# Encoder kernel, layer A: loads and norm in one block, and memory keys and values made in float32 in two places

## The chip, the cores and the metric

The kernel runs on one core of a Trainium2 chip. The metric is the device time of one execution in microseconds (us), as the median of several; less is better. The span is what the profiler sees of one execution, from its first to its last instruction.

## What is computed

```python
def layer_a(x, mem, ln_g, w_in, mem_ln_g, w_mem, w_out):
    h = rms_norm(x, ln_g)
    z = h @ w_in
    ...
    y_mix = dilated_mixer(qkv).astype(x.dtype)
    y_mem = memory_attention(q_mem, rms_norm(mem, mem_ln_g), w_mem)
    y = jnp.concatenate([y_mix, y_mem], axis=-1) * jax.nn.silu(gate)
    return x + y @ w_out

def memory_attention(q, mem_n, w_mem):
    kv = mem_n @ w_mem
    kh = kv[..., :MEM_WIDTH].reshape(Bn, M, MEM_HEADS, HEAD_DIM)
    vh = kv[..., MEM_WIDTH:].reshape(Bn, M, MEM_HEADS, HEAD_DIM)
    s = jnp.einsum('bshe,bmhe->bhsm', qh, kh).astype(F32) * (HEAD_DIM ** -0.5)
    p = jax.nn.softmax(s, axis=-1)
    o = jnp.einsum('bhsm,bmhe->bshe', p.astype(vh.dtype), vh)
```

Two sequences (prompt and sample) of 512 tokens with 1024 features go through layer A (three dilated attentions and an attention over 256 memory rows per sequence) and layer B (gated linear attention and the same memory attention with weights of its own), and a last norm. The memory attention has 4 heads of 128.

## The kernel before

Tokens and features stand transposed, features in the 128 partitions, in 8 chunks of 128 (`KC`). All is float32. The large products are not made in float32 but with every operand split into a high and a low part of type fp32r: ScalarE (ACT) copies the high part, VectorE (DVE) or GpSimd (POOL) subtracts it from the operand to get the low one, and TensorE (PE) makes three products, high by high, high by low, low by high. Small products (scores, transposes, weighted values) are plain float32 matmuls; the profile counts two MATMUL records for each of them, but one for a transpose.

The order is written out by hand, engine by engine, with semaphores. Stages are blocks: a stage begins when all engines and the queues have ended the one before.

1. `load_and_transpose`. SP loads 12 tiles of 128 rows, four of memory and then eight of tokens, into three buffers. PE transposes each, ACT squares it for the sum of squares (L391), and ACT (L392) and DVE (L400) each move a half out of PSUM. The memory tiles are scaled by their norm on DVE (L417). POOL issues the loads of the five gains and of `onorm` (L346, L347), which add to the semaphore `const_in`. SP stores both to DRAM (L334, L337).
2. `norm_a`. DVE computes the norm factors of all 8 token tiles, spreads them over the partitions with PE (L657, L625), scales the tokens (L639), and forms sums of token quarters, since the projection uses a Strassen-like scheme with 7 products for 8 (`OPS`). ACT makes the high parts (L601), DVE and POOL share the low parts (L587) and the sums, and PE makes the 7 products of the first pair of weight columns (L301 to L303).
3. `dilated`. 44 pairs of columns, 7 products each; attention is woven in. The last four pairs belong to the memory heads: their queries and gates.
4. `memory_a`. SP loads the normed memory; DVE multiplies each chunk by the gain (L1386), ACT and DVE split it (L1319, L1389). For each head PE makes keys and values transposed (`unit`, L198 to L200, four times 24 matmuls of width 256), ACT moves them out (L1298), PE turns the values (L1229). For each of four groups of 256 queries: scores (L1210), softmax on DVE and ACT (L1344 to L1356, L1277), transposes of the probabilities (L1221), and per sequence the weighted values (L1237). DVE multiplies by the gate (L1364) and SP stores y (L1188).
5. The output projection of layer A begins (L1749, L1801), then layer B, whose memory stage `memory_b` has the same steps as 4 (gain: L1679, low part: L1682).

## Time and profile before

| | us |
|---|---|
| median of 3 runs | 2252.23 |
| lowest and highest | 2248.18, 2253.43 |
| the profiled execution | 2254.23 |
| its span | 2252.6 |
| PE busy | 2094.9 (93%) |
| DVE busy | 1177.1 (52%) |
| ACT busy | 839.6 (37%) |
| POOL busy | 525.8 (23%) |

Busy time counts instructions, not waits. PE's ends are modelled, so its share is an upper bound. A stage can be far from the mean: what bounds it is read from the waits in it. The granted clock of PE has two levels, 1.2 and 2.4 GHz, shown as 0.5 and 1.0 of full speed.

### The profile page before, as it was taken

Reading aid. Unit: us, or ns where it says so; the run is one execution under the profiler, and the core shown is the slowest. Engines: PE = TensorE matmul, PEld = TensorE weight load, DVE = VectorE, ACT = ScalarE, POOL = GpSimd, SP = SyncE. Lnnn points to the kernel's source line nnn. Section 1 sums busy time; section 2 is a strip of 40 time slices with the busy share of each in tenths; the row PEclk is TensorE's granted clock in tenths of the full one; section 3 lists DMA queues with packets and bytes.
Section 4 is the critical chain, followed back from the end, with each engine's and each line's share of the span. In section 5 each row is a group of like instructions: output and inputs, shape, how many; then the busy total and the mean of one; then the engine's idle time right before and its main releaser. Section 6 shows DMA issues by size and latency. Waiting matters only on the chain. (4 is left out here: it accounts for less than half of the span.)

```text
span 2252.6 us, 29111 instructions
## 1 busy us (share of the span) xinstructions
PE 2094.9 (93%) x10172; PEld 1707.4 (76%) x10172; DVE 1177.1 (52%) x2047; ACT 839.6 (37%) x1518; POOL 525.8 (23%) x394
## 2 busy tenths in 40 slices
PE   5799999999999999999987998999898987998998
PEld 4578888787888788888776786778787875886786
DVE  6755464647363645555344434576868583433423
ACT  5333443434253434343344312343434442334310
POOL 4623232323232222323100023132323231000010
PEclk7899999999999999999989998999999998999998
DMA  7122222121112112212123522210101012222612
GB/s 263 42 57 62 57 57 70 47 70 52 61 51 74 47 59 59 64 56 62 54 91 103 160 67 101 71 29 20 57 19 56 19 37 75 63 60 63 189 56 93
DMA packets 210834, 157.21 MB, mean 70 GB/s; under 512 B 8625, under 2 KB 196305, under 8 KB 210514
## 3 DMA queue, kind: packets, MB, share of 16 engines
q1 hardware_dynamic: 205842, 147.68, 21.7%
q0 software_dynamic: 4928, 8.70, 1.6%
q8 instruction: 37, 0.61, 0.1%
q14 instruction: 27, 0.22, 0.0%
HBM read 128.99 MB, written 27.36 MB: 69 GB/s over the span
## 5 line engine op out<-in xcount | busy, mean ns | idle before, releaser
L274 DVE TENSOR_TENSOR w_lo<-w_raw,w_hi 128x512 fp32r<-128x512 f32 x303 | 271.8, 898 | 354.6 <-ACT w_hi L270 354.0
L198 PE MATMUL z_ps<-b_parts,w_hi 128*128 128x512 f32 x656 | 271.0, 413 | 20.4 <-ACT g_gate L208 12.3
L270 ACT ACTIVATE w_hi<-w_raw 128x512 fp32r<-128x512 f32 x308 | 192.5, 626 | 229.3 <-PE z_ps L303 101.6
L200 PE MATMUL z_ps<-b_parts,w_lo 128*128 128x512 f32 x656 | 265.4, 405 | 0.0
L301 PE MATMUL z_ps<-ah_hi,w_hi 128*128 128x512 f32 x608 | 249.1, 410 | 11.6 <-DVE ah_lo L587 9.0
L303 PE MATMUL z_ps<-ah_hi,w_lo 128*128 128x512 f32 x608 | 243.2, 400 | 0.0
L302 PE MATMUL z_ps<-ah_lo,w_hi 128*128 128x512 f32 x608 | 242.4, 399 | 0.0
L199 PE MATMUL z_ps<-b_parts,w_hi 128*128 128x512 f32 x560 | 228.0, 407 | 0.0
L183 DVE TENSOR_TENSOR w_lo<-w_raw,w_hi 128x1024 fp32r<-128x1024 f32 (+1 forms) x65 | 119.4, 1837 | 140.4 <-ACT w_hi L179 139.9
L198 PEld LDWEIGHTS z_ps<-b_parts,w_hi 128*128 128x128 f32 x656 | 128.5, 196 | 55.2 <-issue 25.2
L2121 POOL TENSOR_TENSOR g_E<-g_E,g_q 128x1024 f32<-128x1024 f32 x28 | 91.2, 3259 | 292.1 <-ACT g_E L2323 278.1
L301 PE MATMUL t_ps<-ah_hi,w_hi 128*128 128x512 f32 x352 | 144.6, 411 | 8.0 <-DVE ah_lo L587 6.6
L200 PEld LDWEIGHTS z_ps<-b_parts,w_lo 128*128 128x128 f32 x656 | 127.8, 195 | 30.6
L301 PEld LDWEIGHTS z_ps<-ah_hi,w_hi 128*128 128x128 f32 x608 | 116.1, 191 | 39.4 <-issue 10.8
L303 PE MATMUL t_ps<-ah_hi,w_lo 128*128 128x512 f32 x352 | 140.4, 399 | 0.0
L302 PE MATMUL t_ps<-ah_lo,w_hi 128*128 128x512 f32 x352 | 140.3, 399 | 0.0
L303 PEld LDWEIGHTS z_ps<-ah_hi,w_lo 128*128 128x128 f32 x608 | 115.9, 191 | 27.8
L302 PEld LDWEIGHTS z_ps<-ah_lo,w_hi 128*128 128x128 f32 x608 | 116.5, 192 | 25.2
L249 POOL TENSOR_TENSOR w_raw<-w_raw 128x512 f32<-128x512 f32 x44 | 57.1, 1298 | 322.9 <-DMA w_raw<-in_a_win 316.7
L199 PEld LDWEIGHTS z_ps<-b_parts,w_hi 128*128 128x128 f32 x560 | 110.0, 196 | 23.6
L736 ACT ACTIVATE qkv<-z_ps 128x512 f32<-128x512 f32 (+2 forms) x132 | 65.5, 515 | 152.6 <-PE z_ps L303 151.2
L301 PE MATMUL s_ps<-ah_hi,w_hi 128*128 128x512 f32 x272 | 111.4, 409 | 1.8 <-DVE ah_lo L587 1.8
(418 smaller groups left out, 4372.5 us busy)
## 6 DMA issues: line engine op xcount, KB each, us to landing
w_raw<-in_a_win SPq DMA_DIRECT2D x220, 256.0 KB, 3.0
w_raw<-in_b_win SPq DMA_DIRECT2D x33, 512.0 KB, 4.1
y_scratch<-y SPq DMA_DIRECT2D x16, 512.0 KB, 2.8
w_raw<-in_a_wout SPq DMA_DIRECT2D x8, 768.0 KB, 5.7
w_raw<-in_b_wout SPq DMA_DIRECT2D x8, 768.0 KB, 6.1
xt_scratch<-work SPq DMA_DIRECT2D x2, 2048.0 KB, 10.6
w_raw<-in_a_wmem SPq DMA_DIRECT2D x8, 512.0 KB, 4.5
ares<-xt_scratch POOLq DMA_DIRECT2D x8, 512.0 KB, 3.8
```

The lines of the kernel that those rows point to most:

```text
L183: dve.tensor_tensor(w_lo[slot][:, 0:nk, :], w_raw[slot][:, 0:nk, :], w_hi[slot][:, 0:nk, :].bitcast(F32), ALU.subtract).then_inc(lo_done, 1)
L198: pe.matmul(z_ps[s][:, 0:width], w_hi[slot][:, k, :], hi[k][:, tok], start=(k == 0), stop=False)
L199: pe.matmul(z_ps[s][:, 0:width], w_hi[slot][:, k, :], lo[k][:, tok], start=False, stop=False)
L200: mm = pe.matmul(z_ps[s][:, 0:width], w_lo[slot][:, k, :], hi[k][:, tok], start=False, stop=(k == nk - 1))
L249: pool.tensor_tensor(raw["X"], raw["A21"], raw["A22"], ALU.add).then_inc(s_sum, 1)
L270: act.activation(op_ring(w_hi, u), op_raw[i], ACT.Copy).then_inc(hi_op, 1)
L274: eng.tensor_tensor(op_ring(w_lo, u), op_raw[i], op_ring(w_hi, u).bitcast(F32), ALU.subtract).then_inc(lo_op, 1)
L301: pe.matmul(out, a_hi[:, k, :], h_hi[:, i, k, :], start=first, stop=False, skip_group_check=True)
L302: pe.matmul(out, a_hi[:, k, :], h_lo[:, i, k, :], start=False, stop=False, skip_group_check=True)
L303: mm = pe.matmul(out, a_lo[:, k, :], h_hi[:, i, k, :], start=False, stop=(k == 3), skip_group_check=True)
L736: part = act.activation(o, b, func)
L2121: pool.tensor_tensor(E[n % 2][:, 0, :], E[n % 2][:, 0, :], a[:], ALU.mult).then_inc(op_done, 1)
```

## The change

- The stages 1 and 2 become one block, `prologue`. The eight token tiles are loaded first, then the four of memory, into four buffers; the norm factors are made in three groups: prompt, sample, memory. Low parts and token sums are all on DVE and twice as wide (128x1024). ACT issues the two stores of the tokens itself, after tile 4 and after tile 7. The memory tiles are moved out of PSUM by ACT alone; they are stored without the norm, and the spread norm factors are stored too (`m_row_scratch`).
- The memory keys of layer A are made in the same block, as plain float32 products of the weights `wk` and the normed memory, width 512, one head behind each of the products 1 to 4 (`keys`), and stored (`k_scratch`).
- In the last stretch of `dilated`, SP loads memory, keys and norm factors into `work`, and DVE scales the memory there (`memory_row`).
- `memory_a` has no splitting and no keys left; the values are made in float32 directly by token (`values`: memory as the stationary operand, weights of width 128), a quarter of a head beside each group of scores.
- `memory_b` applies norm factor and gain in one instruction with two operands in SBUF and waits for one load more.

```diff
+        def prologue(xa, qkv, h_hi, h_lo, early, st):
...
+            @block.sync
+            def _(sp):
...
+                for t in range(NT):
+                    row(t)
+                pair_load(sp, A["a_win"][0], (0, DIL_W), 0)
+                for t in range(NT, N):
+                    row(t)
+                for h in range(MEM_HEADS):
+                    sp.dma_start(wk[h], w_view(A["a_wmem"][0], h * HD)).then_inc(wk_in[h], 16)
...
+                sp.dma_start(mt_scratch, mt).then_inc(mt_stored, 16)
...
+            @block.gpsimd
...
+                op_split_lo(pool, 0, 0, 0)
+                for n in range(1, 5):
+                    weight_sum(pool, 0, n)
+                for i in range(1, RING):
+                    op_split_lo(pool, 0, i, i)
+                for n in range(1, 5):
+                    weight_sum(pool, 1, n)
...
+                def keys(h):
+                    pe.wait_ge(wk_in[h], 16)
+                    need(pe, kv_moved, h)
+                    out = (s_ps, t_ps)[h % 2]
+                    for k in range(KC):
+                        if h == 0:
+                            pe.wait_ge(mg_done, k + 1)
+                        mm = pe.matmul(out[:, 0:MT], wk[h][:, k, :], mt[:, k, :], start=(k == 0), stop=(k == KC - 1))
...
+                for t in range(6):
+                    turn(t)
+                spread(0)
+                turn(6)
+                turn(7)
+                spread(1)
+                one(0)
+                for t in range(NT, N):
+                    turn(t)
...
+                for i in range(1, OPS):
+                    one(i)
+                    if i <= MEM_HEADS:
+                        keys(i - 1)
...
+                start(1)
+                store(1)
+                op_split_hi(act, 0, 0, 0)
                 high(0)
+                row(NT, True)
+                op_split_hi(act, 0, 1, 1)
+                row(NT + 1, True)
+                high(5)
+                op_split_hi(act, 0, 2, 2)
+                row(NT + 2, True)
+                row(NT + 3, True)
+                start(2)
...
+                row(6)
                 dve.wait_ge(const_in, 16 * 6)
...
+                scale(0, 0)
+                row(7)
+                variance(1)
                 lows(0)
+                refine(1)
+                scale(1, 0)
+                scale(0, 1)
+                sums_of(1)
+                lows(5)
+                variance(2)
+                scale(1, 1)
+                refine(2)
                 lows(1)
+                sums_of(2)
                 lows(2)
+                memory_rows()
                 lows(3)
+                sums_of(4)
                 lows(4)
+                sums_of(6)
...
                         if m == 0:
                             store(H8 - 1)
+                            for part, there in zip(memory_views(work), (mt_scratch, k_scratch, m_row_scratch)):
+                                sp.dma_start(part, there).then_inc(mem_in, 16)
...
+                            if gating and 2 * OPS <= u < 2 * OPS + KC:
+                                memory_row(u - 2 * OPS)
...
+                    def values(h, m):
...
+                        for k in range(KC):
+                            mm = pe.matmul(z_ps[h % 2][:, m * HD:(m + 1) * HD], m_g[:, k, m * P:(m + 1) * P],
+                                           w_raw[h % 2][:, k, :], start=(k == 0), stop=(k == KC - 1))
...
                     for h in range(MEM_HEADS):
                         for n in range(4):
-                            c = n // 2
-                            unit(pe, C0 + 2 * h + c, c, n % 2, m_hi, m_lo, width=NMEM,
-                                 arrival=ml_done if h == 0 and n == 0 else None)
...
+                            scores(h, n)
+                            values(h, n)
                             if h > 0:
                                 rest(h - 1, n)
+                            if n >= 2:
+                                turn_probs(h, n - 2)
...
-                            dve.tensor_scalar(m_g[k % 2][:], m_hat[:, k, :], gains[:, 2 * i + 1, k:k + 1], None, ALU.mult)\
+                            dve.scalar_tensor_tensor(out=m_g[k % 2][:], in0=m_hat[:, k, :], scalar=gains[:, 2 * i + 1, k:k + 1],
+                                                     in1=m_row[:], op0=ALU.mult, op1=ALU.mult)\
                                 .then_inc(mg_done, 1)
```

The order of instructions, first DVE in the block of the loads. L657 moves token tiles out of PSUM, L683 scales, L712 makes low parts; this is the change's order around its wait for `const_in`:

```order
L670 TENSOR_SCALAR an_diag<-ident,an_rstd 128x128 x3
L657 COPY work<-t_ps 128x4x4x32 [waits pro_turned]
L657 COPY work<-s_ps 128x4x4x32 [waits pro_turned]
L683 SCALAR_TENSOR_TENSOR qkv<-work,gains,o_ps 128x512 [waits pro_row_done,const_in]
L683 SCALAR_TENSOR_TENSOR qkv<-work,gains,o_ps 128x512 x3
L657 COPY work<-t_ps 128x4x4x32 [waits pro_turned]
L661 TENSOR_SCALAR an_var<-an_sums 128x4 [waits pro_sq_done]
L712 TENSOR_TENSOR ah_lo<-qkv,ah_hi 128x1024 [waits pro_hh_done] x2
```

Before, that wait stood at the first instruction of `norm_a`, behind all 12 tiles; now the scaling of the first quarter stands between tiles 6 and 7, and the last token tile and the variance of the sample behind it.

Next PE in the same block, in the change, at the end of product 1 (L310 to L312), the keys of head 0 (L535) and the begin of product 2:

```order
L310 MATMUL t_ps<-ah_hi,w_hi 128x512 [waits pro_hl_done]
L311 MATMUL t_ps<-ah_lo,w_hi 128x512
L312 MATMUL t_ps<-ah_hi,w_lo 128x512
L535 MATMUL s_ps<-qkv,wk 128x512 [waits pro_mg_done,pro_wk_in0]
L535 MATMUL s_ps<-qkv,wk 128x512 [waits pro_mg_done] x7
L310 MATMUL z_ps<-ah_hi,w_hi 128x512 [waits pro_hl_done,dil_lo_op,dil_z_act]
```

Product 2 followed product 1 directly before; now eight float32 matmuls of width 512 stand between them, and so behind the products 2, 3 and 4.

Last PE in the memory stage, first before (one half of a head; L198 to L200 are keys or values), then the change:

```order
L1210 MATMUL s_ps<-akT,qkv 128x256 x2
L198 MATMUL z_ps<-am_hi,w_hi 128x256
L199 MATMUL z_ps<-am_lo,w_hi 128x256
L200 MATMUL z_ps<-am_hi,w_lo 128x256
L198 MATMUL z_ps<-am_hi,w_hi 128x256
```

```order
L1251 MATMUL s_ps<-work,qkv 128x256 x2
L1260 MATMUL z_ps<-w_raw,work 128x128 x8
L1272 MATMUL t_ps<-ident,apm 128x128 x4
L1280 MATMUL o_ps<-apmT,avm 128x512 x2
L1251 MATMUL s_ps<-work,qkv 128x256 x2
L1260 MATMUL z_ps<-w_raw,work 128x128 x8
```

Behind each pair of scores stand eight float32 matmuls of width 128 in place of 24 of width 256 in fp32r, and the stage begins with scores.

## Rows read from the trace of the kernel before

**Rows 1.** Windows: stretch, busy time and count of PE, PEld, DVE, ACT, POOL; clock; DMA
```profile
35.00:97.00 62.00, 34.38 (x102) 23.37 (x103) 58.18 (x64) 24.52 (x47) 44.36 (x30) 0.72 0.27 100
...
70.00:80.00 10.00, 6.55 (x23) 3.56 (x21) 10.00 (x10) 5.11 (x10) 10.00 (x7) 1.00 0.00 0
```
**Rows 2.** Issues to DMA: the last small load of POOL, with its time to landing
```profile
23.19 0.71 POOL L347 DMA_DIRECT2D onorm<-in_b_onorm  x1
...
onorm<-in_b_onorm POOLq DMA_DIRECT2D x1, 1.0 KB, 5.8
```
**Rows 3.** Timeline (start, length in us): the first scaling of `norm_a`
```profile
45.66 2.71 DVE L639 SCALAR_TENSOR_TENSOR work<-work,gains,o_ps 128x512 f32<-128x512 f32 x4
```
**Rows 4.** Groups of DVE, 35 to 97 us: count, busy us, mean ns, idle before
```profile
L587 DVE TENSOR_TENSOR ah_lo<-work,ah_hi 128x512 fp32r<-128x512 f32 x11 | 16.2, 1513 | 0.0
L657 DVE TENSOR_SCALAR y<-ident,an_rstd 128x128 f32<-128x128 f32 x8 | 7.9, 1052 | 0.0
...
L583 DVE TENSOR_TENSOR work<-work 128x512 f32<-128x512 f32 x4 | 2.5, 678 | 0.0
```
**Rows 5.** Groups of ACT, 0 to 35 us, and ACT and DVE at 128x1024
```profile
L391 ACT ACTIVATE squares<-rows 128x1024 f32<-128x1024 f32 x12 | 12.6, 1053 | 5.1 <-DMA rows<-in_mem_prompt 2.8 <-DMA rows<-in_x_sample 1.3 <-DMA rows<-in_x_prompt 1.0
L392 ACT ACTIVATE work<-s_ps 128x512 f32<-128x512 f32 x4 | 2.4, 597 | 1.0 <-PE s_ps L362 1.0
...
1114.43 1.06 ACT L179 ACTIVATE w_hi<-w_raw 128x1024 fp32r<-128x1024 f32 x1 [2.21 <-PE t_ps L303]
...
1120.66 1.22 DVE L183 TENSOR_TENSOR w_lo<-w_raw,w_hi 128x1024 fp32r<-128x1024 f32 x1
```
**Rows 6.** Timeline of PE: two matmuls of a product after an idle time, two in `dilated`
```profile
62.50 0.63 PE L302 MATMUL t_ps<-ah_lo,w_hi 128*128 128x512 f32 x1
62.93 0.63 PE L303 MATMUL t_ps<-ah_hi,w_lo 128*128 128x512 f32 x1
...
1122.20 0.40 PE L302 MATMUL z_ps<-ah_lo,w_hi 128*128 128x512 f32 x1
1122.43 0.39 PE L303 MATMUL z_ps<-ah_hi,w_lo 128*128 128x512 f32 x1
```
**Rows 7.** Timeline: the end of `norm_a` on DVE and the first matmul of `dilated`
```profile
89.87 0.67 DVE L745 TENSOR_TENSOR qkv<-qkv,s_ps 128x512 f32<-128x512 f32 x1
...
96.63 0.47 PE L301 MATMUL z_ps<-ah_hi,w_hi 128*128 128x512 f32 x1 [2.57 <-PEq L1894]
```
**Rows 8.** Windows of the memory stage, columns as in group 1
```profile
1122.80:1128.00 5.20, 0.02 (x1) 0.00 (x0) 0.00 (x0) 2.40 (x3) 0.00 (x0) 0.98 0.42 110
1128.00:1148.80 20.80, 12.60 (x49) 10.57 (x50) 10.03 (x17) 6.36 (x10) 0.00 (x0) 0.51 0.38 125
...
1168.30:1188.80 20.50, 20.50 (x143) 18.08 (x141) 10.61 (x26) 9.43 (x26) 0.00 (x0) 1.00 0.27 78
...
1210.00:1231.10 21.10, 16.21 (x92) 11.86 (x90) 9.92 (x26) 6.68 (x22) 0.00 (x0) 1.00 0.22 62
```
**Rows 9.** Timeline of PE in the memory stage, merged, two records for a float32 matmul
```profile
1152.54 2.09 PE L1210 MATMUL s_ps<-akT,qkv 128*128 128x256 f32 x8
1154.28 0.47 PE L198 MATMUL z_ps<-am_hi,w_hi 128*128 128x256 f32 x1
...
1161.92 1.04 PE L1221 MATMUL t_ps<-ident,apm 128*128 128x128 f32 x8
...
1166.95 1.88 PE L1237 MATMUL o_ps<-apmT,avm 128*128 128x512 f32 x4
```
**Rows 10.** Timeline: the last store of the memory stage
```profile
1231.07 0.36 SPq L1188 DMA_DIRECT2D y_scratch<-y  x1
```
**Rows 11.** Timeline of PE in layer B: eight float32 matmuls of width 128
```profile
1689.45 1.95 PE L2188 MATMUL t_ps<-g_E 128*128 128x128 f32 x16
```
**Rows 12.** `memory_b`: the gain on DVE, and PE behind the low parts
```profile
L1679 DVE TENSOR_SCALAR g_gate<-bm_hat,gains x8: 476/480/486, 1900.4 to 1913.5; 128x512 f32<-128x512 f32 x8
...
1911.84 0.39 PE L198 MATMUL z_ps<-bm_hi,w_hi 128*128 128x256 f32 x1 [1.17 <-DVE bm_lo L1682]
```

More of the change, by code:

```diff
@@ L594, in _, with row @@
             @block.scalar
             def _(act):
-                root_start(act, rstd[:], var[:], var_done, root, 1)
-                def high(o):
-                    for k in range(4):
-                        operand_ready(act, o, k)
-                        act.activation(h_hi[:, o, k, :], place[o][k], ACT.Copy).then_inc(hh_done, 1)
-                for i in range(RING):
-                    op_split_hi(act, 0, i, i)
-                high(0)
-                high(1)
-                evict_act(act, qkv, 0, 0, 0, True)
+                def row(t, both=False):
+                    act.wait_ge(row_in[t % NR], 16 * (t // NR) + 16)
+                    need(act, sq_done, t)
+                    act.activation(y[:], rows[t % NR], ACT.Square, accum_out=sums[:, t:t + 1]).then_inc(sq_done, 1)
+                    evac(act, lambda o, i: act.activation(o, i, ACT.Copy), t, 0)
+                    if both:
+                        act.wait_ge(moved[1], t)
+                        evac(act, lambda o, i: act.activation(o, i, ACT.Copy), t, 1)
@@ new lines, in store, with start @@
+                def store(s):
+                    for b in range(2):
+                        act.wait_ge(moved[b], 4 * s + 4)
+                    tok = slice(s * SEQ, (s + 1) * SEQ)
+                    act.dma_start(xt_scratch[:, :, tok], xa[:, :, tok]).then_inc(x_stored_half[s], 16)
+                def start(g):
+                    root_start(act, rstd[:, GROUPS[g]], var[:, GROUPS[g]], var_done, root, g)
+                def high(o):
+                    for b in range(2):
+                        operand_ready(act, o, b)
+                        if o == 4:
+                            act.wait_ge(turned, N)
+                        if o == 6:
+                            act.wait_ge(kv_done, MEM_HEADS)
+                        act.activation(h_hi[:, o, 2 * b:2 * b + 2, :], place[o][:, 2 * b:2 * b + 2, :], ACT.Copy).then_inc(hh_done, 1)
@@ new lines, in _ @@
+                act.preload_act_table_set("natural_log_exp_and_others")
+                for t in range(5):
+                    row(t)
+                start(0)
+                store(0)
+                for t in range(5, NT):
+                    row(t)
+                start(1)
+                store(1)
+                op_split_hi(act, 0, 0, 0)
+                high(0)
+                row(NT, True)
+                op_split_hi(act, 0, 1, 1)
+                row(NT + 1, True)
+                high(5)
@@ L619, in _ @@
                     op_split_hi(act, 1, i, 7 + i)
-            @block.tensor
-            def _(pe):
-                for t in range(NT):
-                    pe.wait_ge(diag_done, t + 1)
-                    pe.matmul(banks[t // 4][:, t % 4 * P:(t % 4 + 1) * P], ones[:], diag[:, t, :], start=True, stop=True)\
-                        .then_inc(row_done, 1)
-                for i in range(OPS):
-                    product(pe, h_hi, h_lo, 0, 0, i, i, arrival=lambda o, k: low_ready(pe, o, k))
             @block.vector
@@ L654, in _, with row @@
[L654 to L665 removed]
+                def row(t):
+                    evac(dve, lambda o, i: dve.tensor_copy(o, i), t, 1)
@@ new lines, in _ @@
+                dve.memset(eps_col[:], EPS).then_inc(eps_set, 1)
+                for t in range(4):
+                    row(t)
+                variance(0)
+                row(4)
+                refine(0)
+                row(5)
+                row(6)
+                dve.wait_ge(const_in, 16 * 6)
+                scale(0, 0)
+                row(7)
+                variance(1)
+                lows(0)
+                refine(1)
+                scale(1, 0)
+                scale(0, 1)
+                sums_of(1)
```

589 lines of the change are left out of this document (241 added, 348 removed).

## The prediction

> **What bounds the kernel now.** I read the page's 40 slices first, to find where PE is idle or its clock low; then windows of those stretches, then groups and single instructions in them. PE is filled to nine tenths nearly everywhere but in the first slices and near half the span. The long middle, 96.6 to 1122.8 us, is bound by PE and untouched apart from work that lies beside it. So the change is decided in two places, with a third in layer B.
>
> First place, the start. From 35 to 97 us DVE is busy 58.2 of 62 us and PE 34.4: DVE sets the pace [rows 1]. A low part of 128x512 costs it 1.51 us, a token sum of the same shape 0.68 where POOL is quiet [rows 4]: DVE and POOL hinder each other. The first scaling starts at 45.66 [rows 3], behind the barrier of the load stage and 8 factor diagonals that take 7.9 us [rows 4].
>
> Second place, the memory stage. After the last product PE has one matmul in 5.2 us, then works 12.6 of 20.8 us at clock 0.51, fed chunk by chunk; then it is full, with 20.5 us per head at clock 1.00; in the last 21.1 us it works 16.2 [rows 8]. The last store is issued at 1231.1 [rows 10]: the stage lasts 1231.1 - 1122.8 = 108.3 us.
>
> **The change, step by step.**
>
> *The gate at the start.* The new order scales the first quarter behind tile 6, but waits for all six small loads. The last of them is issued at 23.2 and lands 5.8 us later [rows 2], and POOL's order up to it is the same. DVE, through with tile 6 by about 20 (four buffers; ACT needs 1.05 for the square and 0.60 for its half of the move per tile [rows 5]), stands still until **29.0**. That is still 16.7 us before 45.66.
>
> *From 29.0 to the keys,* a chain over four engines:
> - DVE: four scalings of 0.68 (2.71 for four [rows 3]), a move of 0.69, a variance of 0.2: 32.6.
> - ACT: root 0.4, issue of the second store (0.6, my estimate of an issue with an empty queue), high part of a weight 0.6, first half of the high part 1.06 [rows 5]: 35.3; DVE behind its second half, 1.22 [rows 5]: 37.6. Refined root and four diagonals without POOL, 1.7: 39.3.
> - PE has been idle since 20, so I take the lower level: four spreads 1.7, then product 0 as 12 matmuls of 0.43, the distance of two neighbours after an idle time (62.50, 62.93), where it is 0.23 at the upper level [rows 6]: 5.1. That gives 46.1. Only then come the transposes of the four memory tiles, which stand behind product 0 in PE's queue.
> - ACT now moves both halves of a memory tile: 1.05 + 2 x 0.60 = 2.3 us each [rows 5], and has two high parts of weights (1.2) and high part 5 (2.1) between them: the last sum of squares is ready at about 56.6. DVE waits there.
> - DVE: variance 0.2, four scalings 2.7, root and diagonals 1.7, then low part 1, sum 2 and low part 2 at 2.3 each (two halves): 68.1. The store of the memory tiles, issued at 57.6, is in by then, as 2 MB need some 8 us.
>
> *The keys.* Gain and factor go chunk by chunk at 0.7 us, faster than PE takes them. A float32 matmul of width 256 takes 1.74 / 4 = 0.43 us [rows 9], so one of width 512 takes 0.86, 8 of them 6.9 and four heads **27.5**. Between them stand the products 2 to 5 at 2.8 (12 x 0.23): 11.2. PE is then the bound, and the sum 68.6 + 38.7 = 107.3. Low part 6 waits for the last keys through ACT, and DVE's last addition of the pair starts at 109.3. Before, that addition stood at 89.9 and the first matmul of `dilated` at 96.6 [rows 7]; what lies between is the same: 109.3 + 6.7 = 116.0. The start is **19.4 us longer**. It is not longer by DVE: without the keys it would be shorter.
>
> *The lock.* DVE's low parts at 1.51 against 0.68 and its diagonals at 1.05 us each [rows 4] show it waiting for POOL's instructions. POOL now has 13 such instructions in the block, and in the chain above they hold DVE up by 1.8 us, which is in the terms. The Trainium skill says it more sharply (SBUF — State Buffer, Who interferes with whom): whoever starts first holds the port pair for the whole instruction, and the other is blocked. By that rule all 13 could stand in DVE's way; that is a rival below.
>
> *Moves without a price, and what hides them.* The memory's three loads (3.3 MB, some 9 us of the DMA engines) go in front of the weight loads on SP's queue, in the first of the last four pairs; a pair lasts 7 x 2.8 = 20 us and its weights are asked for three products ahead of use. If that cover were gone, up to 9 us. Eight scalings on DVE there, 0.7 each (up to 1.5 beside POOL), lie beside products. One barrier less is already in the start at 29.0. The value weights and the output weights are loaded one stage step earlier than used.
>
> *The memory stage.* Per head, at the upper level: scores 8 x 0.43 = 3.4, values 32 x 0.22 = 7.2 (8 of width 128 take 1.95 less a tail of 0.16 [rows 11]), transposes 1.7, weighted values 3.4 (two of width 512 take 1.88 with their tail, 1.7 without [rows 9]). Sum 15.7, for 20.5 before [rows 8]. DVE and ACT need under 7 us per head. The stage starts with scores, about 1.5 us after the last product; four heads are 62.8; at the end the last head's transposes and weighted values wait for ACT's move of the values and for DVE's split of the first output weights, which I walk through as 3.7 us more. 1.5 + 62.8 + 3.7 = 68.0, against 108.3: **40.3 us shorter**. Of these, 19 are the four heads, the rest is the start: no loads, no splitting, no lower clock.
>
> Is it less work for PE? Hardly: keys 6.9 and values 7.2 per head stand against about 11.9. The Trainium skill (FP8 and Floating Point Precision, TensorE Precision Notes) says that true FP32 goes through the array in 4 passes, where the split form here takes 3. By that rule alone keys and values would be a third dearer, 15.3 per head, and the sum 5 us worse. The rows decide for 14.1.
>
> *Layer B.* The gain costs 0.48 us per chunk [rows 12]; with a second tensor it is like the scaling of the tokens, 0.68 to 0.73. PE waits for these low parts at the end [rows 12], so 8 x 0.22 = 1.8 lies on the path, and the load in front adds 0.9: **2.7 us longer**, between 1 and 4.
>
> **The sum.** 19.4 - 40.3 + 2.7 = -18.2. The span 2252.6 becomes 2234.4, the profiled execution 2254.2 becomes 2236.0, and the median, 2.0 under the profiled one, 2252.2 - 18.2 = **2234**.
>
> **Bounds.** The start: 12 longer if PE stays at the upper level and POOL never meets DVE; 31 longer if the small loads land 9 us later and the lock costs a little more. The memory stage: 36 to 42 shorter. Layer B: 1 to 4. All good ends together -29, all bad ones -1.
>
> **The rivals.**
> 1. *PE's clock during the keys; slower than before.* If PE stands at the lower level from the keys on, the 38.7 us of keys and products become about 75, and the result is -18 + 36 = +18: **2270**. It turns to a loss once half of that stretch runs at the lower level. For it: after idle times PE ran at 0.43 per matmul [rows 6], and it is idle for some 9 us before product 1. Against: from 70 to 80 us the clock was 1.00 with PE busy only 6.6 of 10 us [rows 1], and the keys stand back to back. 0.07.
> 2. *The memory stage is not bound by PE.* Each of the 16 groups has scores, maximum, exponential, reciprocal, scaling, transpose, about 4.9 us in a row against PE's 3.9. If they hardly overlap, the stage is 16 us longer: **2250**. Against: the softmax of a group has two slots until PE turns it. 0.08.
> 3. *The small loads land later,* because the token stores run beside the tile loads: +9 us in front of everything: **2243**. Against: POOL's issues are 5 us apart before and hardly depend on other queues. 0.10.
> 4. *The lock holds DVE at every POOL instruction:* 13 x 1.26 less the 1.8 that I have: +14, **2248**. Against: most of them fall where DVE waits anyway. 0.07.
> 5. *The start is cheaper,* as ACT and PE reach the memory tiles earlier: 10 us less, **2224**. 0.08.
>
> **The numbers.** My forecast has 0.60. About 0.2% (4.5 us) is what a measurement of this kernel can tell from no change: faster is below 2247.7, slower above 2256.7. Faster: 0.60, rivals 3 and 5 and half of 2 and 4, near 0.84, less 0.02 for what I have not thought of. Slower: rival 1 and 0.01 more. The range 2222 to 2250 takes in the bounds and rivals 2 to 5, and leaves out rival 1 and the far ends.
>
> **What the profile will show.** Right: DVE idle from about 20 to 29 with `const_in` behind it; the first product of `dilated` at 116 with keys back to back at clock 1.00; the memory stage 68 us long, clock 1.00 from its start, 15.7 us per head; layer B's memory stage 2 to 3 us longer. Wrong: keys at 1.7 us per matmul (rival 1); PE idle between scores in the memory stage (rival 2); the first scaling far from 29 (rival 3); DVE's halves at 2 us and more all along (rival 4); a gap in the last pairs of `dilated` would mean that the memory's loads are not hidden.

## The result and the profile after

The changed kernel takes **2232.9 us** (median of 4 runs, 2231.9 to 2234.2); the kernel before, run beside it on the same chip, 2250.2 (2247.6 to 2253.4). The ratio is 0.9928, 95% interval [0.9908, 0.9949]: 12 to 21 us faster. The forecast was 2234.

The profiled executions are 2252.6 and 2230.2 us long. I cut both at the same five points, each an instruction that both kernels have. The cuts after the change, in the first column of a timeline: first product of `dilated` 124.97, last product over at 1143.9, last store of the memory stage issued at 1213.78, first load of `memory_b` at 1870.58, first product of the last projection at 2066.18.

| stretch | before, us | after, us | difference | forecast |
|---|---|---|---|---|
| start, up to the first product of `dilated` | 96.6 | 125.0 | +28.4 | +19.4 |
| `dilated` | 1026.2 | 1018.9 | -7.3 | 0 |
| memory stage of layer A, last product to last store | 108.3 | 69.9 | -38.4 | -40.3 |
| from there to `memory_b` | 662.8 | 656.8 | -6.0 | 0 |
| `memory_b` | 193.9 | 195.6 | +1.7 | +2.7 |
| rest | 164.8 | 164.0 | -0.8 | 0 |

The total is as forecast, its parts are not: the start is 9 us dearer, and 14 us came from stretches that the change hardly touches. First the places that the prediction named. Windows of the changed kernel, columns as in [rows 1] (PE, PEld, DVE, ACT, POOL; then clock, DMA share, GB/s):

```profile
20.00:32.00 12.00, 0.35 (x4) 0.11 (x2) 0.21 (x1) 1.63 (x4) 2.47 (x3) 0.74 1.06 383
32.00:45.00 13.00, 0.00 (x0) 0.00 (x0) 7.44 (x9) 3.98 (x7) 4.79 (x3) 0.50 1.08 297
...
80.00:110.00 30.00, 30.00 (x88) 16.31 (x87) 14.42 (x17) 6.18 (x9) 1.27 (x1) 1.00 0.13 43
...
1144.00:1150.00 6.00, 4.54 (x34) 4.30 (x33) 2.18 (x6) 3.42 (x7) 0.00 (x0) 1.00 0.00 0
...
1165.80:1181.60 15.80, 15.80 (x105) 13.41 (x104) 7.49 (x22) 6.53 (x22) 0.00 (x0) 1.00 0.23 68
...
1197.40:1213.00 15.60, 12.16 (x65) 8.10 (x63) 6.83 (x16) 6.84 (x17) 0.00 (x0) 1.00 0.30 84
```

All engines stand nearly still from 20 to 32 us while the DMA engines are full. From 80 to 110 PE is busy without a gap at the upper clock. The memory stage is full at 15.8 us per head, where [rows 8] have 20.5 and a start at clock 0.51.

Timeline of the same kernel, four engines (start, length in us; in brackets the idle time before and who ended it):

```profile
7.92 0.91 POOL L497 DMA_DIRECT2D gains<-in_a_mln  x1 [5.38 <-issue]
...
28.68 0.71 POOL L498 DMA_DIRECT2D onorm<-in_b_onorm  x1
...
35.02 2.72 DVE L683 SCALAR_TENSOR_TENSOR qkv<-work,gains,o_ps 128x512 f32<-128x512 f32 x4 [14.82 <-DMA onorm<-in_b_onorm]
...
40.96 3.66 DVE L712 TENSOR_TENSOR ah_lo<-qkv,ah_hi 128x1024 fp32r<-128x1024 f32 x2 [2.54 <-ACT ah_hi L599]
44.55 1.22 DVE L104 TENSOR_TENSOR an_tmp<-an_rstd 128x4 f32<-128x4 f32 x1
...
55.57 0.60 ACT L578 ACTIVATE qkv<-s_ps 128x512 f32<-128x512 f32 x1 [12.65 <-PE s_ps L515]
...
124.97 0.77 PE L310 MATMUL z_ps<-ah_hi,w_hi 128*128 128x512 f32 x1 [4.25 <-PEq L1887]
...
1146.46 1.95 PE L1260 MATMUL z_ps<-w_raw,work 128*128 128x128 f32 x16
```

The last small load is issued at 28.7 instead of 23.2 [rows 2], and the first scaling starts at 35.0, not at the 29.0 of the prediction. The two halves of low part 0 take 3.66 us while POOL works on weight sums, and a DVE instruction on 4 columns 1.22, whose neighbours take 0.16. POOL's sums beside them:

```profile
43.68 2.06 POOL L262 TENSOR_TENSOR w_raw<-w_raw 128x512 f32<-128x512 f32 x1
...
45.88 1.26 POOL L266 TENSOR_TENSOR w_raw<-w_raw 128x512 f32<-128x512 f32 x1
```

In layer B the gain with the norm's factor in it:

```profile
1877.34 0.75 DVE L1667 SCALAR_TENSOR_TENSOR g_gate<-bm_hat,gains,bm_row 128x512 f32<-128x512 f32 x1 [3.13 <-DMA bm_hat<-mt_scratch]
1878.79 0.69 DVE L1671 TENSOR_TENSOR bm_lo<-g_gate,bm_hi 128x512 fp32r<-128x512 f32 x1 [0.70 <-ACT bm_hi L1596]
1879.40 0.75 DVE L1667 SCALAR_TENSOR_TENSOR g_gate<-bm_hat,gains,bm_row 128x512 f32<-128x512 f32 x1
```

Chunks come 2.06 us apart, 0.27 more than the 1.79 before, where the gain took 0.48 [rows 12].

### The profile page after: what moved, and what is told of

It is laid out like the page before. It is cut to its first block and busy times, and to the rows that moved or that the text cites. A ratio compares the mean times of both kernels' runs of the same rounds, so it can differ in the third digit from the quotient of the medians.

```text
span 2230.2 us, 28839 instructions
## 1 busy us (share of the span) xinstructions
PE 2075.2 (93%) x10092; PEld 1688.7 (76%) x10092; DVE 1152.6 (52%) x2025; ACT 825.5 (37%) x1487; POOL 501.6 (22%) x375
## 5 line engine op out<-in xcount | busy, mean ns | idle before, releaser
L310 PE MATMUL z_ps<-ah_hi,w_hi 128*128 128x512 f32 x608 | 247.2, 407 | 5.0 <-PEq L1887 4.3
L312 PE MATMUL z_ps<-ah_hi,w_lo 128*128 128x512 f32 x608 | 241.3, 397 | 0.0
L192 DVE TENSOR_TENSOR w_lo<-w_raw,w_hi 128x1024 fp32r<-128x1024 f32 (+1 forms) x57 | 109.4, 1919 | 125.4 <-ACT w_hi L188 124.9
L310 PE MATMUL t_ps<-ah_hi,w_hi 128*128 128x512 f32 x352 | 143.8, 409 | 0.4 <-DVE ah_lo L712 0.4
L312 PE MATMUL t_ps<-ah_hi,w_lo 128*128 128x512 f32 x352 | 139.6, 397 | 0.0
L310 PEld LDWEIGHTS z_ps<-ah_hi,w_hi 128*128 128x128 f32 x608 | 115.6, 190 | 30.2 <-DVE w_lo L283 4.7
L312 PEld LDWEIGHTS z_ps<-ah_hi,w_lo 128*128 128x128 f32 x608 | 115.0, 189 | 26.8
L310 PE MATMUL s_ps<-ah_hi,w_hi 128*128 128x512 f32 x272 | 111.1, 409 | 0.0
```

What stands on the lines that cost most here:

```text
L192: dve.tensor_tensor(w_lo[slot][:, 0:nk, :], w_raw[slot][:, 0:nk, :], w_hi[slot][:, 0:nk, :].bitcast(F32), ALU.subtract).then_inc(lo_done, 1)
L310: pe.matmul(out, a_hi[:, k, :], h_hi[:, i, k, :], start=first, stop=False, skip_group_check=True)
L312: mm = pe.matmul(out, a_lo[:, k, :], h_hi[:, i, k, :], start=False, stop=(k == 3), skip_group_check=True)
```

## The experiments

Two questions: why the start is 9 us dearer than worked out, and where the other 13 us came from. Each time of "the dilated stage" below is that of its first product, 96.6 before and 125.0 after the change. That time scatters: the start of the kernel is the same code in the changed kernel and in e6, e10 and e12, and took 125.0, 128.6, 125.5 and 124.9 us in their profiled executions. So a difference of less than some 4 us between two starts counts only where rows show the place at which it arises.

### e1: the first scaling waits for its own gain only

```
-  pool.dma_start(gains[:, i, :], ...).then_inc(const_in, 16)
+  pool.dma_start(gains[:, i, :], ...).then_inc(aln_in if i == 0 else const_in, 16)
...
-  dve.wait_ge(const_in, 16 * 6)
+  dve.wait_ge(aln_in, 16)
   scale(0, 0)
...
   def memory_rows():
+      dve.wait_ge(const_in, 16 * 5)
```

> The changed kernel, but the load of layer A's token gain has a semaphore of its own: DVE waits for it alone before the first scaling, and for the other five small loads only before the memory tiles' gain. Theory A (the wait for six small loads stands on the path: DVE idle from 20.2 to 35.0 us): the first scaling starts behind tile 6 near 20.3, and the first product of the dilated stage, at 125.0 in the changed kernel, comes 8 to 14 us earlier, at 111 to 117; the median falls by as much, to 2219 to 2225. Theory B (something else is as late: the weights and the memory tiles come by queues of the same loaded DMA engines, or PE's order with product 0 ahead of the memory tiles): the scaling moves but the dilated stage starts less than 4 us earlier, and the median stays above 2229.

Timeline of this kernel:

```profile
20.23 2.71 DVE L684 SCALAR_TENSOR_TENSOR qkv<-work,gains,o_ps 128x512 f32<-128x512 f32 x4
...
26.21 6.60 DVE L713 TENSOR_TENSOR ah_lo<-qkv,ah_hi 128x1024 fp32r<-128x1024 f32 x2 [2.59 <-ACT ah_hi L600]
...
35.93 2.08 PE L522 MATMUL v_ps<-an_diag,ones 128*128 128x128 f32 x8 [15.47 <-DVE an_diag L671]
...
111.94 0.77 PE L311 MATMUL z_ps<-ah_hi,w_hi 128*128 128x512 f32 x1 [4.26 <-PEq L1889]
```

The scaling starts 14.8 us earlier, the dilated stage 13.0. Median 2219.6 (4 runs, 2210.7 to 2231.7), ratio to before 0.9866 [0.9821, 0.9910]; the runs lie so far apart that this interval just touches the changed kernel's, and the 13 us rest on the rows. Theory A holds: the wait for six loads, of which one is needed, lay on the path, and 14.8 us less of it brought 13.0. That the missing 1.8 us came back where POOL's work now meets DVE's low part 0 (6.60 us for the two halves) fits the rows and was not tested by itself.

### e2: the memory tiles ahead of product 0

```
   turn(6)
-  turn(7)
+  for t in range(7, N):
+      turn(t)
   spread(1)
   one(0)
-  for t in range(NT, N):
-      turn(t)
```

On ACT the four memory rows follow tile 7, ahead of the second root, and DVE moves tile 7 ahead of its wait.

> The changed kernel with its gate left alone, but PE turns the four memory tiles ahead of the factors of the second sequence and of product 0, and ACT squares and moves them while DVE waits for the small loads; DVE moves tile 7 ahead of that wait. Theory C (the memory tiles stand on the path: ACT waits 12.65 us for PE with the first of them, and DVE waits 3.4 us for high part 5 and 2.1 us for the last sum of squares): the keys start 4 to 6 us earlier and the dilated stage at 119 to 121. Theory D (DVE's own work is the bound between 49 and 82 us): DVE's idle time only moves, and the stage starts at 123.5 or later.

The dilated stage starts at 120.5, 4.5 us earlier (theory C). The median does not show it: 2235.0, ratio 0.9926 [0.9910, 0.9943], the changed kernel's own ratio. In the profiled execution `dilated` is 5.3 us longer than in that of the changed kernel (1024.2 us), 3.6 us of it idle time of PE, which scatters (see the last experiments). The keys, too, start 4.5 us earlier than in the changed kernel (73.60 for 78.07). So the gain in the start is shown by rows, and one in the time is not.

### e3: two of eight chunks of the keys

```
   for k in range(KC):
...
-      mm = pe.matmul(out[:, 0:MT], wk[h][:, k, :], mt[:, k, :], ...)
+      if k in (0, KC - 1):
+          mm = pe.matmul(out[:, 0:MT], wk[h][:, k, :], mt[:, k, :], ...)
```

> The changed kernel with 2 of the 8 chunks of every head's keys multiplied (the first and the last), so the memory keys are left incomplete. It takes 4 x 6 x 0.86 = 20.6 us from PE in the block. Theory E (from the first keys on the block is bound by PE alone): the dilated stage starts 17 to 20.6 us earlier, at 104.5 to 108, and the start of the kernel is then about 10 us longer than before the change. Theory F (DVE or ACT is nearly as late, keys lie partly in time that is idle anyway): at 110 or later. The memory stage stays at 15.8 us per head.

Timeline:

```profile
76.72 1.10 PE L536 MATMUL s_ps<-qkv,wk 128*128 128x512 f32 x2 [1.34 <-DVE qkv L720]
81.33 1.77 PE L536 MATMUL s_ps<-qkv,wk 128*128 128x512 f32 x2 [3.51 <-DVE qkv L720]
...
108.39 0.47 PE L310 MATMUL z_ps<-ah_hi,w_hi 128*128 128x512 f32 x1 [4.26 <-PEq L1888]
```

The stage starts 16.6 us earlier for 20.6 taken from PE, between theory E (17 or more) and F (15 or less). From the first key to the first product of `dilated` it is 15.2 us less (31.7 for 46.9); the other 1.4 lie ahead of the keys, where the two kernels are the same. With so little work in the first head's keys PE waits 3.5 us for DVE's gain of the last chunk, and from 81 to 86 us its clock is 0.65 in the mean. In the changed kernel PE has no gap between the first key (78.07) and the end of product 5 (116.9): there it is the bound, and E is right in that, while the size shows that DVE is not far behind it. A remark of the prediction falls with this, for the changed kernel as it is: that without the keys the start "would be shorter" than before. With a quarter of them left it is still 11.8 us longer than 96.6; the 6.9 us that are left could bring it to 101.5 at best.

### e4: the first token store 24 us later

```
   start(0)
-  store(0)
...
   start(1)
+  store(0)
   store(1)
```

> The changed kernel with the first store of the tokens (2 MB, issued at 14.4 us) issued just ahead of the second, behind the wait for the small loads. Theory G (the store's traffic makes the small loads slower): the last three small loads are issued 4 to 5 us apart instead of 6 to 7, and the first scaling starts at 29 to 31 instead of 35.0. Theory H (the tile loads with four buffers fill the DMA engines by themselves; the first two small loads were already 6.4 and 6.0 us apart ahead of the store): the first scaling stays within 2 us of 35.

Issues and first scaling:

```profile
13.31 0.88 POOL L497 DMA_DIRECT2D gains<-in_b_ln  x1 [4.72 <-issue]
20.94 0.89 POOL L497 DMA_DIRECT2D gains<-in_b_mln  x1 [6.76 <-issue]
27.74 0.88 POOL L497 DMA_DIRECT2D gains<-in_lnf  x1 [5.91 <-issue]
...
34.90 2.72 DVE L683 SCALAR_TENSOR_TENSOR qkv<-work,gains,o_ps 128x512 f32<-128x512 f32 x4 [16.10 <-DMA onorm<-in_b_onorm]
```

The scaling does not move (34.9), so theory G is out, and H's number holds. Rival 3 of the prediction had the effect right (6 us, not its 9) and the cause wrong. The one run of this kernel took 2243.5 us, 10.7 above the changed kernel's median; 1.4 us of that are in the start and most of the rest in the idle time of `dilated` and in the stretch up to `memory_b`, which scatter. What the loads show is that each of the five gains is issued 0.3 us after the one before has landed: in the changed kernel 6.4 and 6.0 us between the first three, which need 6.1 and 5.7 to land; only `onorm` follows at once (0.9 us). The DMA engines' share from 20 to 32 us is 1.12 even without the store.

H's reason, the four buffers of the tile loads, does not fit all traces. The first two distances add up to 11.0 to 12.2 us in the three traces with the order of before and to 10.9 to 12.7 in the eleven with the change; the next two to 9.8 to 10.8 against 12.9 to 15.2. The extra time lies in the loads issued from some 13 us on, and from 12.7 us on SP issues the weights, which before came at 22.9. So the early loads of weights are the likelier cause; neither they nor the number of buffers was changed by itself.

### e7: POOL's weight sums spread out

On top of e1:

```
   op_split_lo(pool, 0, 0, 0)
-  for n in range(1, 5):
-      weight_sum(pool, 0, n)
-  for i in range(1, RING):
+  weight_sum(pool, 0, 1)
+  op_split_lo(pool, 0, 1, 1)
+  weight_sum(pool, 0, 2)
+  op_split_lo(pool, 0, 2, 2)
+  weight_sum(pool, 0, 3)
+  weight_sum(pool, 0, 4)
+  for i in range(3, RING):
       op_split_lo(pool, 0, i, i)
```

ACT makes high part 3 of the weights after `high(2)` instead of ahead of the factors' row.

> The kernel with the gain's own semaphore (first scaling at 20.2), and POOL's weight sums spread out between its low parts of weights instead of four in a row from 28.2 to 35.3 us, where DVE's two halves of low part 0 took 6.60 us instead of 2.36. Theory K (DVE stands while POOL's instruction runs): low part 0 takes 2.4 to 4 us, PE's factors of the second sequence start at 32 to 34 instead of 35.9, and the dilated stage at 108.5 to 110.5 instead of 111.9. Theory L (the lost time only moves, since each sum holds DVE up wherever it stands): low part 0 is shorter, but the dilated stage starts within 1 us of 111.9.

```profile
26.71 5.42 DVE L717 TENSOR_TENSOR ah_lo<-qkv,ah_hi 128x1024 fp32r<-128x1024 f32 x2 [2.66 <-ACT ah_hi L604]
...
41.26 2.72 DVE L688 SCALAR_TENSOR_TENSOR work<-work,gains,v_ps 128x512 f32<-128x512 f32 x4 [4.92 <-DMA xt_scratch<-work]
...
46.17 4.49 DVE L717 TENSOR_TENSOR ah_lo<-work,ah_hi 128x1024 fp32r<-128x1024 f32 x2
```

Low part 0 is 1.2 us shorter and DVE's next scalings start 2.8 us earlier, but then DVE waits 4.9 us for the store of the tokens (1.5 in e1), and low part 5 takes 4.49 us beside the sums that were moved there (2.36 in e1). The first key starts at 64.0, 1.0 us earlier than in e1. The dilated stage starts at 112.6, against 111.9, because PE runs the first keys at clock 0.55 and 0.59 here and at 1.00 in e1, which costs 1.7 us (see e8). So the number is theory L's, and of the 2.8 us most went where L says; but less than 4 us between two single executions decides little. The one run took 2222.6 us. Moving POOL's work off one place of DVE's chain put most of it on another.

### e8: both edits of e1 and e2

The edit of e1, with the order of e2 on PE; ACT takes the four memory rows right behind high part 0, and DVE makes the memory's factors ahead of low parts 5 and 1.

> Both edits together: the gain's own semaphore, and PE turns all four memory tiles ahead of product 0; ACT squares and moves them from about 30 us on, where it waited 11.6 us for PE, and DVE makes the third variance and the memory's factors ahead of low parts 5 and 1. Theory M (the two add up, 13.0 us and 4.5 us in their own runs): the dilated stage starts at 106 to 108.5. Theory N (with the gate gone, DVE's 40 us of own work and the lock are the bound, and the tiles only fill its last gap of 2.2 us): 109 to 112. The median is as many us below that of the run with the semaphore alone (2219.6), within its scatter.

```profile
28.93 1.97 PE L516 MATMUL s_ps<-ident,rows 128*128 128x128 f32 x8 [8.58 <-DMA rows<-in_mem_prompt]
...
51.00 0.76 PE L311 MATMUL t_ps<-ah_hi,w_hi 128*128 128x512 f32 x1 [2.00 <-DVE ah_lo L710]
60.05 8.80 PE L536 MATMUL s_ps<-qkv,wk 128*128 128x512 f32 x16 [3.59 <-DVE qkv L718]
...
108.64 0.76 PE L311 MATMUL z_ps<-ah_hi,w_hi 128*128 128x512 f32 x1 [4.26 <-PEq L1886]
```

108.6, between the two theories. Up to the first key the two edits add up: it starts at 60.05, 5.0 us earlier than in e1 (65.06), where e2 alone gained 4.5. Of these, 3.3 reach the dilated stage; the other 1.7 go in the first keys. Windows over their first 4 us, e1 and then e8 (PE first; the clock is the third number from the end):

```profile
65.10:67.10 2.00, 2.00 (x5) 0.98 (x6) 2.00 (x4) 1.45 (x2) 1.54 (x2) 1.00 0.17 48
```

```profile
60.10:62.10 2.00, 2.00 (x3) 0.96 (x4) 2.00 (x4) 0.84 (x1) 1.50 (x2) 0.50 0.19 51
62.10:64.10 2.00, 2.00 (x4) 0.73 (x4) 2.00 (x4) 0.00 (x0) 0.74 (x1) 0.65 0.27 80
```

In e8 the first keys run at the lower level of the clock; a head of keys with its product takes 11.4 us instead of 9.7. The same happened in e6 and e7 (1.7 us each), and in no other trace that makes the keys whole. PE had waited 3.6 us for DVE ahead of the first key in e8 and 2.1 in e6, but also 2.1 in e4, which kept the upper level; what decides it is open. PE also still waits for DVE ahead of product 1. Median 2214.8 (2212.4 to 2217.8), ratio 0.9845 [0.9825, 0.9865].

### e6: layer B's gain without the factor

```
-  dve.scalar_tensor_tensor(out=m_g[k % 2][:], in0=m_hat[:, k, :], scalar=gains[...], in1=m_row[:], ...)
+  dve.tensor_scalar(m_g[k % 2][:], m_hat[:, k, :], gains[...], None, ALU.mult)
```

> The changed kernel, but layer B's memory tiles get the gain alone, as before the change; the norm's factor is left out there. Theory (my term for layer B, 8 x 0.27 us of a longer DVE instruction on PE's path): the eight gains take 0.48 us each instead of 0.75, the chunks come 1.78 us apart instead of 2.05, and from the first load of the memory tiles to the end of the last gain's low part it is 2.2 us less. Rival: PE has other work there, and the first instruction behind the chunks moves by less than 1 us.

```profile
1873.46 0.49 DVE L1667 TENSOR_SCALAR g_gate<-bm_hat,gains 128x512 f32<-128x512 f32 x1 [3.23 <-DMA bm_hat<-mt_scratch]
1874.65 0.69 DVE L1670 TENSOR_TENSOR bm_lo<-g_gate,bm_hi 128x512 fp32r<-128x512 f32 x1 [0.70 <-ACT bm_hi L1596]
1875.26 0.48 DVE L1667 TENSOR_SCALAR g_gate<-bm_hat,gains 128x512 f32<-128x512 f32 x1
```

The chunks are 1.8 us apart again. From the stage's first load to the end of the last low part it is 21.9 us for 23.9 in the changed kernel (23.6 to 24.1 in the nine traces with this code), and to the last projection 194.1 for 195.6: 1.5 us of the 2.0 reach the end of the stage. Theory and size hold in the rows; the one run took 2227.6 us.

### e5, e9, e10, e12: the 7 us that no one asked for

In `dilated` both kernels issue the same 4860 matmuls. In its last product pairs they stand back to back; here the first and last of such a stretch, before and after, then in e10 and e12 (described below). Before:

```profile
1096.66 0.40 PE L301 MATMUL z_ps<-ah_hi,w_hi 128*128 128x512 f32 x1
...
1122.43 0.39 PE L303 MATMUL z_ps<-ah_hi,w_lo 128*128 128x512 f32 x1
```

After:

```profile
1117.64 0.39 PE L311 MATMUL z_ps<-ah_lo,w_hi 128*128 128x512 f32 x1
...
1143.67 0.40 PE L312 MATMUL z_ps<-ah_hi,w_lo 128*128 128x512 f32 x1
```

The distance, from the start of one matmul to that of the next, follows: 110 steps in 25.77 us are 234.3 ns each; 112 in 26.03 are 232.4. Over all neighbours of the stage the means are 234.0 and 232.4. The first question was whether that is chance (e5, the kernel before once more):

> The kernel before, unchanged, profiled a second time. In the first two profiles the dilated stage lasts 1026.0 us before the change and 1018.9 after it, with the same instructions; two neighbouring matmuls of a product are 234.0 ns apart before and 232.4 ns after. Theory I (this is the scatter of single executions): here the distance is 232.4 ns or anything else but 234.0, and the stage lasts 1014 to 1024 us. Theory J (it belongs to the program): the distance is again 234.0 ns and the stage lasts 1020 to 1030 us, about 5 us longer than the mean of the four programs with the change (1013.8 to 1024.2).

It was 234.0 again, in every tenth of the stage, and the stage 1033.0 us long (the run took 2254.7): theory J for the distance, while the length also scatters. Comparing where the two programs put the arrays of this stage gave one difference: the kernel before has `x_sums`, 32 bytes per partition, ahead of `ah_hi` and `ah_lo`, and the change removed it, so that these two and the small arrays behind them moved. So e9 lengthened it in the kernel before, and e10 put 32 unused bytes into the changed kernel:

```
-  x_sums = sb("x_sums", [P, NT], stack=st)
+  x_sums = sb("x_sums", [P, 2 * NT], stack=st)[:, 0:NT]
```

```
   with ExitStack() as st:
+      sb("shift", [P, 8], stack=st)
       rows, wk = [], []
```

> The kernel before, but the small array x_sums is 64 instead of 32 bytes long in each partition, so that the token parts ah_hi and ah_lo, which every product reads, begin at a multiple of 64 bytes (110080 and 167424) as they do in the changed kernel (110016 and 167360), and not 32 bytes off one (110048 and 167392). Nothing else differs. Theory O (the place of the token parts sets the distance of two matmuls): 232.4 ns in the dilated stage instead of 234.0, the stage 5 to 12 us shorter than the 1026.0 and 1033.0 of the two profiles of the kernel before, and the median 5 to 12 us below it (ratio 0.995 to 0.998). Theory P (the distance comes with something else of the change, the order of the code for instance): still 234.0 ns, and the median within 3 us of before.

> The reverse: the changed kernel with 32 unused bytes per partition ahead of the token parts, so that these begin at 110048 and 167392, as in the kernel before. Theory O: 234.0 ns, the dilated stage at 1024 to 1033 us instead of the 1013 to 1024 of the changed kernel's kin, and the median at 2238 to 2244 instead of 2232.9. Theory P: 232.4 ns, and the median within 4 us of 2233.

e10, the first and last of 111 steps:

```profile
1125.65 0.40 PE L312 MATMUL z_ps<-ah_hi,w_lo 128*128 128x512 f32 x1
...
1151.66 0.39 PE L312 MATMUL z_ps<-ah_hi,w_lo 128*128 128x512 f32 x1
```

That is 234.3 ns, as before the change. Median 2241.4 (8 runs), ratio to before 0.9953 [0.9937, 0.9968] where the changed kernel has 0.9928. e9 came out between its theories, at 233.2 ns; its median is 7.1 us under before, ratio 0.9971 [0.9956, 0.9986]. That is 3 to 10 us, where 0.8 ns for each of 3612 products are 2.9: the distance explains at most the low end of it. e12 (`[P, 16]` instead of `[P, 8]`) asks whether that middle value belongs to the place:

> The changed kernel with 64 unused bytes per partition ahead of the token parts, which then begin at 110080 and 167424, the places of the aligned kernel of before, where two matmuls were 233.2 ns apart, half way between 234.0 (at 110048) and 232.4 (at 110016). Theory Q (the place alone sets the distance, whatever the program): 233.2 ns here as well, and a median 2 to 5 us above the changed kernel's. Theory R (a multiple of 64 bytes is enough, and the 0.8 ns left belong to the program of before): 232.4 ns, and no difference to the changed kernel.

```profile
1115.66 0.39 PE L312 MATMUL z_ps<-ah_hi,w_lo 128*128 128x512 f32 x1
...
1140.86 0.40 PE L312 MATMUL z_ps<-ah_hi,w_lo 128*128 128x512 f32 x1
```

108 steps of 233.3 ns: theory Q. Its median is 2234.3, ratio 0.9938 [0.9921, 0.9954], 1.5 us above the changed kernel's, less than the 2 to 5 expected and within the scatter. The intervals of e10 and of the changed kernel also overlap, so the distances and the busy times show the effect more firmly than the medians do. Three places, three distances, whichever of the two programs:

| `ah_hi` begins at | kernels | distance, ns | PE busy in `dilated`, us |
|---|---|---|---|
| 110016 | changed, e1 to e4, e6 to e8, e11 | 232.4 | 1009.2 to 1012.4 |
| 110080 | e9, e12 | 233.2 | 1014.8, 1012.5 |
| 110048 | before, e5, e10 | 234.0 | 1016.8, 1017.9, 1015.7 |

The last column is from a window over the stage in each trace; for before, e5 and the changed kernel:

```profile
96.60:1122.80 1026.20, 1016.78 (x4860) 830.63 (x4860) 528.94 (x1186) 398.26 (x863) 277.02 (x240) 1.00 0.21 60
```

```profile
97.30:1130.30 1033.00, 1017.92 (x4860) 829.36 (x4860) 536.72 (x1186) 397.82 (x863) 277.78 (x240) 1.00 0.21 59
```

```profile
125.00:1143.90 1018.90, 1010.77 (x4860) 829.74 (x4860) 531.12 (x1193) 397.13 (x862) 279.52 (x240) 1.00 0.22 64
```

1.6 ns times the 3612 matmuls of products is 5.8 us, the difference of the busy times (6.0). What is left of a window is idle, and that scatters: 9.4 and 15.1 us in two executions of the same kernel, 4.0 to 12.4 in the kernels with the faster place, for the greater part waits of some 1.1 us each for the softmax's maximum. The stretch from the memory stage to `memory_b` scatters alike, 656 to 663 us in three traces (the kernel before twice, and e9), 654 to 662 in the others; its 6.0 us are no gain of the change.

### e11: what could be had

e8, and two orders on DVE: the memory tiles' gain ahead of the last quarter's scaling and sum 2, and in layer B gain k+1 ahead of low part k.

```
   lows(1)
+  memory_rows()
   scale(1, 1)
   sums_of(2)
   lows(2)
-  memory_rows()
...
   for k in range(b * KC // 2, (b + 1) * KC // 2):
-      gain(k)
+      if k == 0:
+          gain(0)
+      if k + 1 < KC:
+          gain(k + 1)
```

> The changed kernel with the gain's own semaphore, the memory tiles ahead of product 0, the memory tiles' gain on DVE ahead of the last quarter's scaling and sum 2, and in layer B the gain of chunk k+1 issued ahead of the low part of chunk k. Against the run with the first two edits (dilated stage from 108.6, median 2214.8) I expect the keys to start at 56 to 57 instead of 60.1, the dilated stage at 104.5 to 106.5, layer B's chunks 1.4 us apart instead of 2.05 (2 to 4 us less there), and a median of 2207 to 2212. Rival: DVE is then late with low part 2 and PE waits between the first keys and product 2, so that the dilated stage starts at 107 or later.

```profile
57.19 7.03 PE L536 MATMUL s_ps<-qkv,wk 128*128 128x512 f32 x16
65.43 0.47 PE L311 MATMUL z_ps<-ah_hi,w_hi 128*128 128x512 f32 x1 [1.22 <-DVE ah_lo L710]
...
105.45 0.77 PE L311 MATMUL z_ps<-ah_hi,w_hi 128*128 128x512 f32 x1 [4.26 <-PEq L1891]
```

Keys at 57.2, the dilated stage at 105.5, layer B's chunks 1.4 us apart, and the time from there to the end 3.7 us less than in the changed kernel. Median **2210.5** (5 runs, 2201.4 to 2212.4), ratio 0.9802 [0.9780, 0.9825]: the fastest of all; the changed kernel, timed in a series of its own, has 2232.9 and 0.9928. It was not run beside e8, so what its last two orders give in the time is not measured by itself. Its dilated stage starts 3.2 us earlier than e8's; the first keys run at clock 1.00 here, which is 1.7 us of that, and PE waits 1.2 us for DVE's low part ahead of product 2.

## Why the prediction was right, and where it was not

**The time** was right to 1 us, with help from outside. The parts that the change was meant to touch give 28.4 - 38.4 + 1.7 = -8.3 us in the traces, not -18.2. About 6 us came from the new place of two arrays. That is 14 of the measured 17; the other 3 are within the interval. e10, the change without that help, has a ratio of 0.9953: 10.6 us faster, between 7 and 14, and a median of 2241.4. So the direction and most of the working were right, and the agreement to 1 us is luck: a start 9 us too cheap in the sum was made good by 6 us from a term that the sum did not have, and by scatter.

**The gate at the start** failed as a step: "POOL's order up to it is the same", and so 29.0. The order was the same, the time of each load was not. The scaling started at 35.0, so 6 us more, and at 34.4 to 36.2 in the six other traces that keep this gate. Why the loads are slower is open; they are so from the one on that is issued beside the weights' loads (e4). The prediction also took the idle stretch in front of it as the price of an order that is still better than before; e1 shows that 13 us of it were to be had for one semaphore.

Rival 5, a start that is cheaper than worked out, is refuted by the same rows.

**The lock**, DVE's waiting for POOL's instructions, was a term of 1.8 us in the chain and too small. Up to the second scaling it cost 1.3 on low part 0, 2.1 on the refined root and 0.9 on the factors' diagonals (3.66 for 2.36, 1.22 and 1.18 for 0.16 each, 1.82 for 0.88), and 1.0 on the memory's diagonals: 5.3 us. That is 3.5 over the term. Together with the gate it makes 9.5, and the keys start 9.5 us later than worked out (78.07 for 68.6), so these two steps are the whole excess. The Trainium skill (SBUF — State Buffer, Who interferes with whom) has it that whoever issues first holds the shared pair for the whole instruction, and the trace agrees: the instruction on 4 columns that starts at 44.55, after POOL's, ends when that one does (45.77 and 45.74 us). Rival 4 with all 13 instructions in DVE's way did not come.

**The keys:** 9.65 us per pair of key and product against 6.9 + 2.8 = 9.7; clock 1.00 throughout, so rival 1 did not come in the changed kernel. A little of it came in e6, e7 and e8, where the first keys ran at the lower level, at a price of 1.7 us and not of 36. PE is the bound, as the stretch without a gap shows.

**The memory stage:** 1.5 us of start as worked out, 15.8 per head against 15.7, and 1.5 us more at the end, where PE waits for the last head's softmax, its move and the output; 69.9 for 68.0. PE was busy in all of 15.80 us, so rival 2 falls. In the last 44 us of `dilated` it was busy throughout, so the memory's loads are hidden as forecast. Eight float32 keys of width 512 take 7.03 us and 32 values some 7.15, together 14.2 for my 14.1. So the rows were the better guide than the four passes against three of the Trainium skill (FP8 and Floating Point Precision, TensorE Precision Notes), by which I had 15.3. (A third more than the prediction's own 11.9 would be 15.9; 15.3 goes by 96 matmuls at 0.119 us, the distance of neighbours there.)

**Layer B:** 1.7 for 2.7, inside its bounds; e6 gives 1.5 for the longer DVE instruction.

**What I had not thought of** is the term of `dilated`. I had called the stage "untouched" and put its term at nothing. Its instructions were the same, but its operands had moved by 32 bytes, and its products take 6 us less.

## What to carry to other kernels

Give a load that something early waits for its own semaphore: a counter shared by six loads makes the first user wait for the last, here 13 us. When work is moved to the front of a kernel, ask which engines then stand still and whether the next tiles could be turned and squared in that time; and a filler that suits one engine's gap may hold up another, as POOL's sums did in both places where they were tried. When two versions differ by less than a per cent, compare the places of the arrays that a long matmul loop reads before crediting the edit, and run the new kernel once with the old places.

## What the hardware showed that I had not expected

- The distance of two back-to-back matmuls of width 512 at clock 1.00 changes with the place of their arrays, here that of the moving operands: 232.4, 233.2 and 234.0 ns at 110016, 110080 and 110048 bytes, the same in two programs, 0.7% of a stage of 1020 us. The two differ by 64 and 32 bytes from the best; both token parts moved together, and the small arrays behind them, so which of them matters, and what rule stands behind the three, is open.
- A small load of POOL's, 4 KB or less, took 4.5 to 5.8 us to land before and 5.7 to 6.7 after the change, and the next gain was issued 0.3 us after that. Without a 2 MB store beside them the last of them landed at 34.9 instead of 35.0 us (e4).
- DVE and POOL hold each other up in both directions: in e8 a DVE instruction on 4 columns took 3.35 us instead of 0.16 beside a low part and then a sum of POOL's, and ended with the second (31.68 and 31.65 us), and one of POOL's took 5.58 instead of 1.27 beside DVE's four halves:

```profile
28.33 3.35 DVE L104 TENSOR_TENSOR an_tmp<-an_rstd 128x4 f32<-128x4 f32 x1
...
47.55 5.58 POOL L284 TENSOR_TENSOR w_lo<-w_raw,w_hi 128x512 fp32r<-128x512 f32 x1 [3.90 <-ACT w_hi L280]
```
